# Attention on one core: VectorE makes the hi parts of a pair's k and q one head sooner

## What is computed

```
z = jnp.einsum('bhqd,bhkd->bhqk', qb, kf)
...
neg_log_keep = jnp.where(mask, jax.nn.softplus(z), 0.0)
rcs = lax.cumsum(neg_log_keep, axis=3, reverse=True)
suffix = jnp.concatenate([rcs[..., 1:], jnp.zeros_like(rcs[..., :1])], axis=-1)
a = jnp.where(mask, jnp.exp(jax.nn.log_sigmoid(z) - suffix), 0.0)
return jnp.einsum('bhqk,bhkd->bhqd', a, vf)
```

## Time and profile before

| | |
|---|---|
| median of three runs | 2016.26 us (2015.67 to 2016.7) |
| the profiled execution, its own time | 2016.22 us |
| its span | 2014.4 us |
| mean granted TensorE clock | 0.99 |
| PE busy | 98% |
| DVE, ACT, POOL busy | 55%, 33%, 7% |
| attention heads | about 1500.6 to 1600 us of the span |

### The profile page before, as it was taken

How to read it: one execution, slowest core, us unless ns; L and a number is a source line. 1 busy time by engine, 2 the same in 40 slices (tenths; PEclk the granted TensorE clock), 3 DMA queues, 4 the chain that set the end, 5 groups by cost and what they waited for, 6 DMA issues and landing times.

```text
span 2014.4 us, 24679 instructions
## 1 busy us (share of the span) xinstructions
PE 1965.3 (98%) x9750; PEld 1593.4 (79%) x9750; DVE 1101.2 (55%) x1344; ACT 661.7 (33%) x742; POOL 144.2 (7%) x96
## 2 busy tenths in 40 slices
PE   6899999999989999999999999999999999999999
PEld 4688888886577888888788888887897887888887
DVE  3766554589877565633666533345559764333322
ACT  3422232242254222222422322224238744223211
POOL 0100000121411000001100000101012120000000
PEclk8999999999989999999999999999999999999999
DMA  9345444526413454433254422232235422222222
GB/s 397 150 170 205 169 186 158 175 91 186 127 53 136 179 196 181 181 121 100 105 201 174 188 98 81 92 124 105 84 84 126 120 89 84 104 88 100 86 89 96
DMA packets 50777, 275.88 MB, mean 137 GB/s; under 512 B 7456, under 2 KB 8096, under 8 KB 25760
## 3 DMA queue, kind: packets, MB, share of 16 engines
q1 hardware_dynamic: 47648, 270.87, 38.0%
q10 hardware_dynamic: 3072, 4.23, 0.8%
HBM read 251.94 MB, written 2.10 MB: 126 GB/s over the span
## 4 chain that ended last, share of the span: by engine, by line
PE 88%; DVE 5%; ACT 3%; DMA 1%; issue 1%; SPq 0%; POOL 0%; DVEq 0%; ACTq 0%
PE ps L1394 27%; PE ps L1395 27%; PE ps L1396 27%; PE ps L1612 2%; DMA stage<-ada_d 1%; DVE w L856 1%; PE ps L1733 1%; PE ps L1747 1%; DVE h_lo L999 1%; ACT h_hi L650 1%; PE ps L1720 1%; PE ps L1501 1%; PE ps L1479 1%; DVE sq_tmp L996 0%; DVE w L1041 0%
## 5 line engine op out<-in xcount | busy, mean ns | idle before, releaser
L1394 PE MATMUL ps<-h_hi,w 128*128 128x512 f32 x1648 | 649.6, 394 | 17.6 <-DVE w L1041 12.9
L1395 PE MATMUL ps<-h_lo,w 128*128 128x512 f32 x1648 | 643.2, 390 | 0.0
L1396 PE MATMUL ps<-h_hi,w 128*128 128x512 f32 x1648 | 642.9, 390 | 0.0
L1394 PEld LDWEIGHTS ps<-h_hi,w 128*128 128x128 f32 x1648 | 310.5, 188 | 95.5 <-DVE w L1041 14.6
L1396 PEld LDWEIGHTS ps<-h_hi,w 128*128 128x128 f32 x1648 | 310.5, 188 | 65.6
L1395 PEld LDWEIGHTS ps<-h_lo,w 128*128 128x128 f32 x1648 | 310.8, 189 | 62.8
L856 DVE TENSOR_TENSOR w<-raw,w 128x1408 fp32r<-128x1408 f32 (+1 forms) x101 | 189.3, 1874 | 210.2 <-ACT w L606 210.2
L606 ACT ACTIVATE w<-raw 128x1408 fp32r<-128x1408 f32 (+1 forms) x101 | 158.9, 1573 | 426.5 <-PE ps L1396 420.6
L1394 PE MATMUL ps<-g_hi,w 128*128 128x512 f32 x704 | 274.2, 390 | 0.0
L1396 PE MATMUL ps<-g_hi,w 128*128 128x512 f32 x704 | 273.9, 389 | 0.0
L1395 PE MATMUL ps<-g_lo,w 128*128 128x512 f32 x704 | 273.9, 389 | 0.0
(11 more groups left out here) (204 smaller groups left out, 1645.5 us busy)
## 6 DMA issues: line engine op xcount, KB each, us to landing
raw<-up_d SPq DMA_DIRECT2D x88, 1024.0 KB, 6.3
ada_raw<-ada_d SPq DMA_DIRECT2D x64, 1024.0 KB, 4.8
raw<-down_d SPq DMA_DIRECT2D x64, 704.0 KB, 4.1
raw<-mix_d SPq DMA_DIRECT2D x28, 1024.0 KB, 4.7
stage<-ada_d SPq DMA_DIRECT2D x12, 1024.0 KB, 20.9
stk<-parted SPq DMA_DIRECT2D x32, 256.0 KB, 4.3
stk<-parted SPq DMA_DIRECT2D x32, 128.0 KB, 2.3
u_blk<-u SPq DMA_DIRECT2D x48, 64.5 KB, 2.0
```

The source lines that it names most:

```text
L1394: pe.matmul(dst, a_hi_, b_hi_, start=start, stop=False, skip_group_check=True)
L1395: pe.matmul(dst, a_hi_, b_lo_, start=False, stop=False, skip_group_check=True)
L1396: return pe.matmul(dst, a_lo_, b_hi_, start=False, stop=stop, skip_group_check=True)
```

## The change

In the loop over the heads, DVE's call of split_qk(c) moves. Before, pairs 2 to 7 were split at the end of heads 1, 3, 5, 7, 9, 11. Now pair 2 is split in head 0, between magnitude(0) and softplus(0, 0), and pairs 3 to 7 at the end of heads 2, 4, 6, 8, 10. The semaphores and their values stay, and so does every other engine's code.

```diff
             for t in range(HEADS):
                 magnitude(t)
+                if t == 0:
+                    split_qk(2)
                 softplus(t, 0)
                 softplus(t, 1)
-                if t % 2 and (t + 3) // 2 < KD:
-                    split_qk((t + 3) // 2)
+                if t and t % 2 == 0 and t // 2 + 2 < KD:
+                    split_qk(t // 2 + 2)
                 if t % 2 and t >= 3:
                     o_low((t - 3) // 2)
```

## The result

The changed kernel takes 2023.67 us in the median of seven runs (2019.23 to 2024.61), against 2016.26 before. The ratio is 1.0032, with an interval of 1.0022 to 1.0042: slower, by about 6.5 us by that ratio (the two medians lie 7.4 us apart, since one of the seven runs was much faster than the others), and outside the range that was forecast, 2017.6 to 2021.3. The profiled execution took 2022.65 us, 6.43 more than the one of before.

What follows compares the result with a forecast made beforehand. PE holds 88% of the chain, but DVE sets the pace in the first heads. Head 4's logits move from 1524.94 to 1528.2, +3.2 us, later pairs 0: 2016.26 + 3.2 = 2019.5 us, range 2017.6 to 2021.3.

Steps and rivals of the forecast that it cites:

- Step 1: DVE behind magnitude 0 in head 0: the casts wait for pair 1's landing, so DVE stands until 1508.35 or so.
- Step 2: Head 0: the cast gets in between POOL's subtractions; sp_hi ends near 1510.57, sp_lo at 1512.1, 0.53 us late.
- rival (d): Head 0's cast waits for both POOL instructions, ending at 1511.9; PE idles 6.0 us; +4.2, 2020.5 us; chance 20%.
- Step 3: Head 0's suffix sums: PE idles 4.7 us, then about 3.4 us of lower clock, putting magnitude 1 at 1515.0.
- Step 4: Magnitude 1 to head 4's logits: 13.16 us instead of 14.58, so PE is ready at 1528.2 instead of 1524.94.
- Step 5: Pair 2's transfer before head 4: landed at 1524.4, needed at 1528.2, so PE's 1.46 us wait is gone.
- Step 6: Five later pairs: POOL holds each odd head's first cast, 0.75 us; at worst 0.6 us in all, taken as 0.
- (a): Pair 1 lands early enough for the casts to fit DVE's 1.48 us wait; 2.9 us sooner, 2013.4 us; chance 5%.
- (e): DVE becomes the bound in the five later pairs, each losing 0.69 us: +3.4, 2022.9 us; chance 10%.
- (c): Head 0: the low clock costs nothing, magnitude 1 at 1513.8; +2.0, 2018.3 us; chance 15%.

## Why the prediction was wrong

**Step 1** held to 0.1 us: the casts start 1508.01 - 1502.20 = 5.81 us behind magnitude 0, forecast 5.86. That wait, with the low clock behind it, is the loss in the heads, as the wait put alone into the kernel before shows.

**Step 2** held for the cast: sp_hi is done 1509.67 + 0.64 - 1502.20 = 8.11 us behind magnitude 0, forecast 8.08, and rival (d) did not occur. The hold of sp_lo was mis-sized: 0.96 us instead of the 0.53 taken, so magnitude 1 could come 0.43 later. The Trainium skill's rule that GpSimd and VectorE contend (GPSIMD Engine Reference, Key points) agrees with this row, an instruction with two SBUF inputs, but it gives no size. For the size I had used the 0.4 us by which other instructions ended behind POOL's, and sp_lo ends 0.8 behind it (1510.35 + 1.92 = 1512.27, POOL at 1508.52 + 2.93 = 1511.45).

**Step 3** was right as far as magnitude 1 and wrong in how long the low clock lasts. Its 1515.0 - 1513.8 = 1.2 us for the low clock are the 12.98 - 11.78 = 1.20 that the version with the clock kept up shows, and magnitude 1 came 12.98 behind magnitude 0 instead of 12.51 for the reason of step 2. But I let the low clock be over by magnitude 1, or nearly, after rows in which PE resumed and then worked without a gap and the clock was back after 3.4 us. Here it was at 0.50 for 8.3 us after the sums began, 3.5 us beyond magnitude 1.

**Step 4** is where the sum failed. Its 13.16 us assumed full clock, so it put the low clock behind magnitude 1 at nothing. It took 1529.69 - 1515.18 = 14.51, with DVE idle 0.75 us before head 1's cast and 0.52 before magnitude 2, both for PE; with the clock kept up it took 13.10. So the heads lost 5.04 to head 4's logits, where I had 3.2: 0.47 more before magnitude 1 (the hold of sp_lo) and 1.35 more behind it (the low clock).

**Step 5** was right: no wait for stk before head 4. **Step 6** was right in mechanism and size: casts of 1.30 us in the odd heads, and the period still 11.87.

**What I had no term for** is the tail, 1.6 us. My sum stopped at head 4 and let the rest of the program move unchanged, and it did not. In the profiled execution the start and the heads alone make -0.29 + 5.09 = 4.80, which would be 2021.0 and just inside the range; the tail's 1.63 took it to 2022.65. The range was made of causes within the heads only and was too narrow at its upper end. None of the rivals (a) to (e) occurred. Rival (e) names a time near the measured one, 2022.9, but by a pair period that grows, and the period stayed at 11.87. Against (c), the clock does cost: 2.6 us as far as head 4.

Why the seven runs lie so far apart (2019.23 to 2024.61) is only partly explained. Low stretches of 3.4 us, which cost 1.5 to 1.6 us each, come and go, and so do waits for stk. Which of them the fastest run lacked, no profile shows.

## What to carry to other kernels

Before an instruction that waits is moved into a gap, add up when what it waits for arrives: the gap of 1.48 us ended 3.7 us before the landing, and since DVE works in order, PE had to stand for it too. A low clock that follows such a stand goes into every later term of the sum, until a row shows that it is over. Where the wait guards a buffer, a second buffer makes the same order pay in the heads (5.09 longer with the wait, 2.41 shorter without), and so does one step later in the order (1.52 shorter). In the whole time neither gain is clear of the scatter. A microsecond or two gained or lost in the middle of a program that PE bounds can be outweighed by a low clock behind an unrelated idle stretch, so measure the stage by its own rows as well as the whole.

## What the runs showed of the hardware

- The lower clock can outlast the idle time by far. Behind 4.7 us of idle time, with resumed sums that still had a gap of 0.30 us and waits on DVE, it was there for 8.3 us after PE resumed (1510.37 to about 1518.7); behind 3.95 us without such a gap, for 5.4.
- Three places of the program (at about 634, 1007 and 1674 us) have PE idle for 2.39 to 2.41 us (2.77 in one profile). In 13 profiles a low stretch of 3.4 us followed 30 times out of 39: 12, 11 and 7 times at the three places. Even an idle stretch of 1.50 us had one once (before head 4 in the kernel before with fillers). The same code had it in one profile and not in another.
- Three DVE instructions with operands in SBUF alone started inside the second of two POOL subtractions, and each ended 0.4 to 0.8 us behind POOL's end: sp_lo took 1.92 us where it takes 0.96 without POOL, a cast to sp_hi 1.31 where it takes 0.56, and with the buffer of its own 1.02. A cast that started 0.2 us before POOL's second subtraction was hardly held: 0.64 beside 0.56.
